# 64x64 products of the RWKV-7 chunk inversion: two batches issued together, the second batch's results in the opposite partition half

## What is computed

```python
def rwkv_scan(r, w, k, v, kk, bb, s0, reverse):
    def step(S, xs):
        rt, wt, kt, vt, kkt, bt = xs
        sa = jnp.einsum('bhvk,bhk->bhv', S, kkt)
        S = S * wt[:, :, None, :] - sa[..., None] * bt[:, :, None, :] + vt[..., None] * kt[:, :, None, :]
        return S, jnp.einsum('bhvk,bhk->bhv', S, rt)
```

## Time and profile before

| | |
|---|---|
| median of 3 runs | 1091.25 us |
| lowest and highest run | 1085.15, 1092.33 us |
| profiled execution, its own time | 1087.14 us |
| its span (first to last instruction on the engines) | 1085.3 us |
| mean granted TensorE clock, 1 being full | 0.973 |
| first layer's recurrent stage | 199.9 to 299.5 us |
| second layer's recurrent stage | 713.6 to 813.0 us |

### The profile page before, as it was taken

One profiled execution on the slowest core, in us unless ns is written; L12 is line 12 of the kernel. 1 busy time (PEld: TensorE's weight loads), 2 busy tenths in 40 slices (PEclk: granted clock), 3 DMA queues, 4 the chain that ended last, 5 costly groups with the idle time before them and its releaser, 6 DMA issues. The chain is left out here.

```text
span 1085.3 us, 25550 instructions
## 1 busy us (share of the span) xinstructions
PE 978.2 (90%) x11105; PEld 705.0 (65%) x11105; DVE 483.0 (45%) x1371; ACT 307.1 (28%) x661; POOL 51.5 (5%) x79
## 2 busy tenths in 40 slices
PE   6899998988879989979989998899888999997786
PEld 4555566788758865645745565778876976664355
DVE  1362388567731343212546156746873252311134
ACT  2330417332221710110153132733322251111000
POOL 0000000000000020012000000000000002000120
PEclk9899999999999999999999999999999999999899
DMA  9759533422168759999742204232027756999993
GB/s 382 304 152 273 157 109 126 157 81 86 66 241 363 293 195 400 378 366 396 318 161 78 77 5 156 88 148 81 8 86 315 306 194 242 393 380 351 381 416 87
DMA packets 43447, 238.74 MB, mean 220 GB/s; under 512 B 5120, under 2 KB 8192, under 8 KB 19904
## 3 DMA queue, kind: packets, MB, share of 16 engines
q1 hardware_dynamic: 29904, 196.37, 47.0%
q0 software_dynamic: 9584, 34.35, 10.5%
q10 hardware_dynamic: 3840, 6.29, 1.8%
HBM read 210.25 MB, written 26.74 MB: 218 GB/s over the span
## 5 line engine op out<-in xcount | busy, mean ns | idle before, releaser
L1030 PE MATMUL bank<-sb_hT,sb_ring 128*128 128x385 f32 (+1 forms) x640 | 206.7, 492 | 4.4 <-ACT sb_hT L1698 4.4
L1030 PEld LDWEIGHTS bank<-sb_hT,sb_ring 128*128 128x128 f32 (+1 forms) x640 | 115.3, 187 | 90.9 <-issue 10.2
L1030 PE MATMUL bank<-sb_arena 64*64 64x64 f32 (+5 forms) x1048 | 102.1, 333 | 9.2 <-DVE sb_arena L2612 3.6
L1698 ACT ACTIVATE sb_u<-bank 128x256 f32<-128x256 f32 (+4 forms) x106 | 48.7, 476 | 204.5 <-PE bank L1030 195.3
L1030 PE MATMUL bank<-sb_ring,sb_arena 128*64 128x256 f32 (+4 forms) x672 | 91.2, 401 | 16.4 <-PEq L1652 10.5
L1030 PE MATMUL bank<-sb_o,sb_ring 128*128 128x257 f32 (+1 forms) x512 | 84.9, 327 | 1.6 <-DVE sb_o L2041 0.9
L1030 PEld LDWEIGHTS bank<-sb_ring,sb_arena 128*64 128x64 f32 (+2 forms) x672 | 56.1, 154 | 44.8 <-issue 33.9
L1030 PEld LDWEIGHTS bank<-sb_o,sb_ring 128*128 128x128 f32 x512 | 77.4, 190 | 10.0 <-issue 2.8
L1030 PEld LDWEIGHTS bank<-sb_arena 128*64 128x64 f32 (+2 forms) x1048 | 58.9, 141 | 35.2 <-issue 22.6
L2041 DVE SCALAR_TENSOR_TENSOR sb_xT<-bank,sb_mod,sb_xT 128x128 f32<-128x128 f32 x144 | 41.1, 345 | 82.3 <-PE bank L1030 81.9
L1030 PE MATMUL bank<-sb_u,sb_arena 64*64 64x64 f32 (+2 forms) x744 | 62.4, 315 | 7.9 <-DMA sb_u<-weights 3.9
(11 more groups left out here) (217 smaller groups left out, 1257.3 us busy)
## 6 DMA issues: line engine op xcount, KB each, us to landing
sb_ring<-weights SPq DMA_DIRECT2D x110, 1024.0 KB, 6.9
sb_arena<-weights SPq DMA_DIRECT2D x37, 1024.0 KB, 20.0
sb_u<-weights SPq DMA_DIRECT2D x18, 1024.0 KB, 12.3
sb_sq<-weights SPq DMA_DIRECT2D x8, 1024.0 KB
sb_hT<-weights SPq DMA_DIRECT2D x8, 1024.0 KB
x_slots<-sb_o POOLq DMA_DIRECT2D x1, 6912.0 KB, 39.4
sb_sq<-x_slots POOLq DMA_DIRECT2D x18, 256.0 KB, 7.6
sb_hT<-x_slots POOLq DMA_DIRECT2D x17, 256.0 KB, 7.7
```

The costliest lines, as they stand in the source:

```text
L1030: return nc.tensor.matmul(out, lhsT, rhs, start=start, stop=stop, skip_group_check=True)
L1698: return nc.scalar.activation(out, in_, func, **kw)
```

## The change

It takes each pair of batches through the inversion together.

- A new TensorE helper `sixteen` issues the products of both batches in turns: per head, batch b on both halves, then batch b+1 on both halves. Batch b's results go to the same half of the partitions as its operands, batch b+1's to the opposite half (`turned`), in two banks. So batch b+1's `power[1]` and `inv[1]` change halves with each step; `inv[1]` starts in the half opposite to the first `power[1]`, where the next power will lie.
- Ones are added to left factors: for batch b+1, `power^T + I` (in `cross[1]` for k = 2 and 3, in `power[1]` itself for k = 4), and for both batches `g4` + I and the identity in the `inv` masks of the crosses. The product then holds the sum already, and the eviction is a plain copy. ScalarE makes these copies for batch b+1 (five more per pair), VectorE for batch b in the merges. In power2 to power4 VectorE still adds for batch b.
- `rw_order` lists each step once per pair. `power1` waits for `matrices_ready` of both batches. Two semaphores are new: `powers_plus_one` (VectorE to TensorE and ScalarE) and `cross_left_ready` (VectorE to TensorE). The `tt` products of `merge0` stay as `eight` for each batch. `values` waits for the last `tt` of both of its batches.
- VectorE starts `inv[1]` with two operations on 64 partitions each, since it crosses halves.

```diff
@@ rw_order
-            out += [(step, first), (step, first + 1)] + SSD_BESIDE.get((first, step), [])
+            out += [(step, first)] + SSD_BESIDE.get((first, step), [])
@@ psum_plan (in part)
             elif step[:5] == "power":
                 k = int(step[-1])
+                if k < 4:
+                    g("v" if k == 3 else "a", "p", l, b + 1, k)
+                    g("a", "p", l, b, k)
                 if k > 1:
                     g("v", "t", l, b, k)
-                if k < 4:
-                    g("a", "p", l, b, k)
+                    g("a", "t", l, b + 1, k)
...
             elif step == "merge0":
                 g("v", "t", l, b, 5)
+                g("a", "t", l, b + 1, 5)
                 g("v", "tt", l, b, 0)
+                g("a", "tt", l, b + 1, 0)
             elif step == "merge1":
                 g("v", "tt", l, b, 1)
+                g("a", "tt", l, b + 1, 1)
@@ TensorE
+            def sixteen(banks_, at, lhsT, rhs, turned=(0, 1)):
+
+                for j in range(4):
+                    last = []
+                    for m in range(2):
+                        for i, q in enumerate(HALVES):
+                            out = HALVES[(i + turned[m]) % 2]
+                            ins = mm(banks_[m][out, at + 64 * j:at + 64 * j + 64], lhsT[m][q, j, :], rhs[m][q, j, :])
+                        last.append(ins)
+                return last
...
-                        pe.wait_ge(matrices_ready, len(RW_BATCHES) * l + b + 1)
+                        pe.wait_ge(matrices_ready, len(RW_BATCHES) * l + b + 2)
+                    if k < 4:
+                        banks_ = [open_bank(pe, "p", l, m, k) for m in pair[::-1]]
+                        if k > 1:
+                            taken(pe, "p", l, b, k - 1)
+                        last = sixteen(banks_, 256, pw[::-1], pwT[::-1], (1, 0))
+                        if k < 3:
+                            last = sixteen(banks_, 0, pwT[::-1], pw[::-1], (1, 0))
+                        for ins in last:
+                            ins.then_inc(psum_filled, 1)
+                    if k > 1:
+                        banks_ = [open_bank(pe, "t", l, m, k) for m in pair]
+                        if k == 4:
+                            for m in pair:
+                                taken(pe, "p", l, m, 3)
+                        else:
+                            pe.wait_ge(powers_plus_one, len(RW_BATCHES) * l + b + k - 1)
+                        if k > 2:
+                            for m in pair:
+                                taken(pe, "t", l, m, k - 1)
+                        for ins in sixteen(banks_, 0, [pwT[0], pwT[1] if k == 4 else cross[1]], inv):
...
+                        pe.wait_ge(cross_left_ready, len(RW_BATCHES) * l + b + 2)
+                    for ins in sixteen(banks_, 0, [g4[m][:, :, 2, :] for m in pair], inv):
+                        ins.then_inc(psum_filled, 1)
...
+                elif step == "merge0":
+                    banks_ = [open_bank(pe, "t", l, m, 5) for m in pair]
+                    taken(pe, "cross", l, b + 1, 0)
+                    taken(pe, "tT", l, b + 1)
+                    for ins in sixteen(banks_, 0, [invT[m] for m in pair], cross):
+                        ins.then_inc(psum_filled, 1)
@@ ScalarE
-                elif step == "power3":
-                    bank = filled(act, "p", l, b, 3)
-                    f(power[s][:, 1, :, :], shaped(bank[:, 256:512], 4, 64), ACT.Copy).then_inc(read("p", l, b, 3), 1)
-                elif step in ("power1", "power2"):
-                    copy(power[s].rearrange("p k j n -> p (k j) n"), "p", l, b, int(step[-1]))
+                elif step[:5] == "power":
+                    k = int(step[-1])
+                    if k == 3:
+                        filled(act, "t", l, b, 3)
+                        bank = filled(act, "p", l, b, 3)
+                        f(power[0][:, 1, :, :], shaped(bank[:, 256:512], 4, 64), ACT.Copy)\
+                            .then_inc(read("p", l, b, 3), 1)
+                    elif k < 3:
+                        for m in (1, 0):
+                            if k == 2 and m == 0:
+                                filled(act, "t", l, b, 2)
+                            elif k == 2:
+                                act.wait_ge(powers_plus_one, len(RW_BATCHES) * l + b + 1)
+                            copy(power[m].rearrange("p k j n -> p (k j) n"), "p", l, b + m, k)
+                    if k > 1:
+                        copy(inv[1], "t", l, b + 1, k)
                 elif step == "transpose":
-                    copy(invT[b], "tT", l, b)
+                    for m in (b, b + 1):
+                        copy(invT[m], "tT", l, m)
+                elif step == "merge0":
+                    copy(inv[1], "t", l, b + 1, 5)
+                    copy(invT[b + 1], "tt", l, b + 1, 0)
+                elif step == "merge1":
+                    copy(invT[b + 1], "tt", l, b + 1, 1)
@@ VectorE
+                taken(dve, "nd", l, b, 1)
+                tt(power[s][:, 1, :, :], g4[b][:, :, 2, :], bc(C("inv")[:, 0:64], 1, 4), ALU.mult)
+                if s == 0:
+                    last = tt(inv[0], power[0][:, 0, :, :], bc(C("ident64"), 1, 4), ALU.add)
+                else:
+
+                    for i, q in enumerate(HALVES):
+                        last = tt(inv[1][HALVES[1 - i]], power[1][q, 0, :, :], bc(C("ident64", q), 1, 4), ALU.add)
+                last.then_inc(matrices_ready, 1)
+
+            def inverse_step(l, step, b):
...
+                    dve.wait_ge(matrices_ready, len(RW_BATCHES) * l + b + 2)
+                    for m in pair:
+                        left = g4[m][:, :, 2, :]
+                        tt(left, left, one, ALU.add).then_inc(cross_left_ready, 1)
...
+                    if k < 4:
+                        if k == 3:
+                            filled(dve, "t", l, b + 1, 2)
+                        taken(dve, "p", l, b + 1, k - 1)
+                        tt(cross[1], power[1][:, 1, :, :], one, ALU.add).then_inc(powers_plus_one, 1)
+                    if k == 3:
+                        bank = filled(dve, "p", l, b + 1, 3)
+                        dve.wait_ge(powers_plus_one, len(RW_BATCHES) * l + b + 2)
+                        tt(power[1][:, 1, :, :], four(bank, 256), one, ALU.add).then_inc(read("p", l, b + 1, 3), 1)
                     bank = filled(dve, "t", l, b, k)
...
+                elif step == "merge0":
+                    bank = filled(dve, "t", l, b, 5)
+                    v.tensor_copy(inv[0], four(bank)).then_inc(read("t", l, b, 5), 1)
+                    bank = filled(dve, "tt", l, b, 0)
+                    v.tensor_copy(invT[b], four(bank)).then_inc(read("tt", l, b, 0), 1)
+                elif step == "merge1":
+                    bank = filled(dve, "tt", l, b, 1)
+                    v.tensor_copy(invT[b], four(bank)).then_inc(read("tt", l, b, 1), 1)
@@ constants
-        "inv": np.concatenate([small(same(16))] + [small(same(2 * n) - same(n)) for n in (16, 32)], 1),
+        "inv": np.concatenate([small(same(16))] + [small(same(2 * n) - same(n) + np.eye(P)) for n in (16, 32)], 1),
```

More of the change, by code:

```diff
@@ L1281, in inverse_step @@
                         pe.wait_ge(factors_ready, 2 * l + 2)
[L1282 to L1301 removed]
+                    for m in pair:
+                        matrices(l, m)
                 elif step[:5] == "power":
@@ L1366, in recurrence_step @@
                     bank = open_bank(pe, "rv", l, q)
-                    taken(pe, "tt", l, batches[1], 1)
+                    for d in range(2):
+                        taken(pe, "tt", l, batches[d], 1)
                     for j in range(4):
@@ L2322, in ssd_step, with matrices @@
                     last.then_inc(read("hst", l), 1)
[L2324 removed]
+            def matrices(l, b):
                 d = RW_BATCHES[b][1]
                 s = b % 2
[L2328 to L2344 removed]
@@ new lines, in matrices @@
+                for half in range(2):
+                    bank = filled(dve, "g4", l, b, half)
+                    mask = bc(bc(C(f"rw{d}"), 1, 2), 1, 2)
+                    tt(g4[b].rearrange("p j (a k) n -> p j a (k n)", k=2)[:, half::2, :, :],
+                       shaped(bank[:, :], 2, 2, P), mask, ALU.mult)\
+                        .then_inc(read("g4", l, b, half), 1)
+                for half in range(2):
+                    bank = filled(dve, "nd", l, b, half)
+                    tt(power[s][:, 0, half::2, :], shaped(bank[:, 0:P], 2, 64), bc(C(f"nd{d}"), 1, 2), ALU.mult)\
+                        .then_inc(read("nd", l, b, half), 1)
@@ new lines, in inverse_step, with four @@
+            def inverse_step(l, step, b):
+                pair = (b, b + 1)
+                one = bc(C("ident64"), 1, 4)
+                def four(bank, at=0):
+                    return shaped(bank[:, at:at + 256], 4, 64)
+                if step == "matrices":
+                    for m in pair:
+                        matrices(l, m)
```

(4 more changed lines are left out.)

152 lines of the change are left out of this document (60 added, 92 removed).

## The result

The changed kernel takes 1094.18 us (median of 20 runs, 1088.07 to 1102.02) against 1090.86 for the kernel before in the same comparison (20 runs). The ratio is taken over all runs and isn't the quotient of the two medians, which is 1.0030; it is 1.0049, interval 1.0031 to 1.0067: slower by 0.3 to 0.7%, where 0.4% faster was forecast. The profiled execution took 1088.07 us and is the fastest of the 20.

A forecast was written before the change was run, and what follows sets the result against it. TensorE, busy 90%, was taken as the bound, with instruction supply limiting its dense stretches. Per layer -2.4 - 0.5 - 0.5 + 1.4 = -2.0 us, for both -4.0, took the median from 1091.25 to 1087.2; range 1077 to 1096.

The forecast's parts named there:

- Faster products: `sixteen`: 2,496 matmuls at 17 ns instead of 29, 30 us less, none of it certain to reach the end.
- The last rival: In `sixteen` the four quadrants don't overlap: 29 ns stay and waits come in, +17 us, 1108; chance 0.07.
- First pair: First pair of batches, each layer: -0.9 to the transposes, -1.9 behind, +0.4 for masks at merge1, sum -2.4 us.
- the wait for both masks: First pair's joined `power1`: VectorE's last operation becomes two, so it starts 0.35 us later, at 206.70 instead of 206.35.
- Pairs 2 and 4: Second and third pairs: dense stream turns most gain into "issue" gaps; -0.5 us each, bounds +1 and -3.
- Added work: ScalarE's five more copies per pair, 0.39 us each, and VectorE's additions, its count staying: no term of their own.
- The clock: Empty 2.8 us ahead of `power1`: about one more half-clock stretch per layer, +1.4 us each.
- third rival: The clock falls behind every `matrices`, all six pairs: 9.0 us instead of 2.8, 1093.5, slightly slower; chance 0.11.
- Supply: Dense TensorE stretches: instructions for 126 matmuls take some 4 us, limiting the gain; "issue" waits grow beyond 10 us per layer.

The follow-up runs named there:

- serial: The changed kernel with the sixteen products issued batch by batch instead of in turns, two quadrants busy at a time: 1095.16 us, 1.0041 to the kernel before.
- serial_split: split with the sixteen products issued batch by batch, so two quadrants work at a time: 1090.94 us, 1.0016 to the kernel before.
- first_only: The kernel before with the change's scheme in the first pair of each layer alone: 1089.22 us, 1.0012 to the kernel before.
- split: The changed kernel with `power1` taken batch by batch as each one's masks are done, other steps still in pairs: 1090.81 us, 1.0004 to the kernel before.
- wait_both: The kernel before with one edit, `power1` of a pair's first batch waiting for VectorE's masks of both batches: 1097.50 us, 1.0066 to the kernel before.
- rest_only: The kernel before with the change's scheme in the second and third pairs only: 1094.20 us, 1.0046 to the kernel before.
- rest_own: rest_only with each batch of those pairs waiting for its own operands alone and issued by itself at every step: 1095.64 us, 1.0066 to the kernel before.
- warm: The changed kernel with three overwritten 128x385 products in TensorE's wait ahead of each `power1`: 1096.96 us, 1.0073 to the kernel before.
- warm_first: The changed kernel with three overwritten 128x385 products only ahead of the first pair's `power1`: 1094.37 us, 1.0042 to the kernel before.
- dup: The changed kernel with every `sixteen` behind `power1` in the second and third pairs issued twice: 1132.84 us, 1.0392 to the kernel before.

## Why the prediction was wrong

- **Faster products.** Right: 29 ns became (0.69 - 0.22) / 31 = 15 ns, and TensorE's busy time fell by 29 us. The last rival (no overlap) was wrong, and the trace disagrees with the rule on one bank beside it (the Trainium skill, "TensorEngine Tiling (Array Packing)", Restrictions and Gotchas): the products overlap with both halves writing one bank, each into its own half of the partitions. That little of the 30 us would reach the end was right: serial and serial_split put the overlap at 0 to 2 us, within noise of some 3 us.
- **First pair, -2.4 us.** In the profile it was -1.5 and -2.9, the size forecast. Over the runs it was nothing (first_only: +0.7 a layer, -0.7 to +2.0). The term that failed is the wait for both masks, priced at 0.35 us: split's `power1` in that pair turns 1.0012 into 0.9978 and 0.9959, 1.8 to 2.9 us per layer, and wait_both shows the price in the kernel before, 1.2 us a pair. `power1` of the first batch had been useful work in VectorE's time. In the profile the wait makes `power1` 0.5 us late; where the rest of its price arises isn't shown.
- **Pairs 2 and 4 (the second and third), -0.5 us each.** This is the step that failed most, by sign: rest_only gives +5.0 us over four pairs, +1.2 each, just past the bound of +1. It was summed from TensorE's side: waits shortened by faster products, less a late `power1`, with the supply as a ceiling that takes the gain and costs nothing itself. The four versions of these pairs, with and without the joined `power1`, the overlap and the other joined waits, all lose 0.46 to 0.66%, so what the change costs there is neither of the two terms. In rest_own, with products at the old rate, the supply waits of the first layer's second pair still grow, from 0.6 to 2.7 us.
- **Added work, at nothing.** This is the other half of the same failed step. "Its count stays" is true, but what rest_own kept is just this work (copies, additions, the split mask) with the opposite halves and a new order, and it costs the whole loss. Only 1.1 us of it in the first layer's second pair can be put down to an engine, the split mask's and the copy's; none of TensorE's seven idle waits there ends with an addition. The rest shows as "issue", and its cause stays open.
- **The clock, +2.8 us for both layers.** The mechanism was seen, and its extent undersized: half clock in both stages went from 6.8 to 23.9 us, in all six pairs as the third rival had it, and over the runs the clock fell by 0.015. That rival's time, 1093.5, is the nearest to 1094.2, but warm and warm_first gave back most of the mean clock and none of the time, and wait_both loses more than the change with 0.013 more clock. So that rival hit the number and is not shown as the cause; neither is it excluded as a part of it, since the fillers didn't clear the stages of half clock.
- **Supply.** The 126 matmuls in some 4 us came back in the profiles of the change and of dup, most of the "issue" time in the two stages ends 1.2 to 1.8 us behind an instruction packet, and an added matmul that takes 15 ns costs 27 to 29: the count of instructions, not array time, is paid. The expected growth of "issue" came too, 9.9 to 16.8 us.

In the sum: for both layers -4.0 was forecast, and by the runs the first pairs gave +1.3 instead of -4.8 and the others +5.0 instead of -2.0, the clock's +2.8 included in what was measured (6.3 together, against 5.3 by the ratio of the whole change). The stated range held the time (1094.2 in 1077 to 1096); the side was wrong.

## What to carry to other kernels

Before making an engine faster, measure what one more of its instructions costs at the end: here a matmul of 15 ns cost 27 to 29, and 30 us of array time were worth 0 to 2, at the most 5. Joining two batches under one wait gives away the work that the first did while the second was being prepared: it cost 1.2 us a pair in the kernel before, and in the change it was paid in the first pair and not measurably in the others. Added copies, additions and a new order can't be put at nothing because their engine has idle time: in pairs 2 and 3 they cost 1.2 us a pair with no engine's queue to show for most of it. Before calling a queue the cause, compare the end of the suspected operation with the start of what reads it.

## What was not expected of the hardware

Products of four quadrants in turns, both halves writing each of two banks, run at about twice the rate of two quadrants: 0.69 us for 32 matmuls against 1.15. An idle wait that the profile calls "issue" mostly ends 1.2 to 1.8 us behind the end of a 16,384-byte instruction packet (20 of 27 in dup). Executions of one kernel with a lower mean clock are slower: over 20 runs of the change the time falls by about 470 us for a clock higher by 1, and in the five sets of runs of before by 310 to 800, which is 0.14 to 0.37 us for each us at half clock (310 / (2 x 1090) and 800 / (2 x 1090)). That holds only from run to run of one kernel: between kernels a higher mean clock came with a longer time (warm, 0.968 and 1097.0; the change, 0.954 and 1094.2).
